# Order of 32-row groups per expert: 3, 3, 2, 2, 3, 3 in place of 3, 3, 2, 3, 3, 2

## The reference

```python
logits = (xt @ w_router) + b_router
top_val, top_idx = lax.top_k(logits, TOP_K)        # 4 of 32 experts for each token
gates = jax.nn.softmax(top_val, axis=-1)
...
hid = x_pad[toks] @ w1[e] + b1[e]                  # w1[e]: 1024 x 2048, float32, 8 MB
glu = jnp.minimum(hid[..., :D_FF], SWIGLU_LIMIT)
lin = jnp.clip(hid[..., D_FF:], -SWIGLU_LIMIT, SWIGLU_LIMIT)
act = glu * jax.nn.sigmoid(SWIGLU_ALPHA * glu) * (lin + 1)
y   = (act @ w2[e] + b2[e]) * wts[:, None]         # w2[e]: 1024 x 1024, float32, 4 MB
```

## Time and profile before

| | |
|---|---|
| median of three runs | 1705.96 us |
| the profiled execution's own time | 1706.75 us |
| its span (first to last instruction) | 1705.0 us |
| PE busy over the span | 1593.5 us, 93% |
| matmuls with w1 (line 2337), 5376 of them | 612.2 us busy, 61.5 idle before them |
| matmuls with w2 (line 2349), 5376 of them | 296.5 us busy, 1.8 idle before them |
| DMA, last slices before the end | 9 tenths or more busy, 403 to 430 GB/s |
| chain that ended last | PE 71%, DMA 26% |

### The profile page before, as it was taken

The page is one execution under the profiler, slowest core; times in us unless marked ns, Lnnn a source line. Parts: engine busy times, 40 slices in busy tenths (PEclk is TensorE's granted clock), DMA queues, the critical chain, the costliest instruction groups (busy, mean ns, idle before and its releaser), DMA issues.

```text
span 1705.0 us, 32935 instructions
## 1 busy us (share of the span) xinstructions
PE 1593.5 (93%) x14089; PEld 819.2 (48%) x14089; DVE 646.2 (38%) x1131; ACT 202.3 (12%) x434; POOL 369.4 (22%) x416
## 2 busy tenths in 40 slices
PE   7999999999999998999989898989899998989886
PEld 5776767566668855343433333433333333433334
DVE  5565457455463535541322221312213222313125
ACT  2211012222120011010000000000100000100001
POOL 1521122111027613212121121121211211211201
PEclk9999999999999998999999999999999999999999
DMA  7442434111125353899999999999999999999996
GB/s 261 147 136 70 145 101 105 45 37 52 37 100 141 112 234 142 316 404 420 427 424 427 421 422 407 410 422 430 421 404 427 425 426 403 415 427 426 423 428 268
DMA packets 91968, 498.19 MB, mean 292 GB/s; under 512 B 9280, under 2 KB 58672, under 8 KB 74000
## 3 DMA queue, kind: packets, MB, share of 16 engines
q1 hardware_dynamic: 78304, 463.06, 67.2%
q0 software_dynamic: 13040, 32.61, 5.6%
q10 hardware_dynamic: 496, 0.56, 0.1%
HBM read 477.56 MB, written 23.89 MB: 294 GB/s over the span
## 4 chain that ended last, share of the span: by engine, by line
PE 71%; DMA 26%; issue 1%; DVE 1%; SPq 0%; ACT 0%; POOL 0%; POOLq 0%; ACTq 0%; DVEq 0%
PE PS L2337 26%; DMA ring<-in_w 23%; PE PS L519 12%; PE PS L2349 6%; PE PS L2218 6%; PE PS L2123 3%; PE PS L2243 3%; PE PS L2083 3%; PE PS L2163 2%; PE PS L2047 2%; PE PS L2183 2%; DMA ring<-y_dram 1%; PE PS L2167 1%; PE PS L2152 1%; PE PS L1922 1%
## 5 line engine op out<-in xcount | busy, mean ns | idle before, releaser
L2337 PE MATMUL PS<-ring,mix_sb 128*32 128x512 f32 x5376 | 612.2, 614 | 61.5 <-DMA ring<-in_w 60.6
L2337 PEld LDWEIGHTS PS<-ring,mix_sb 128*32 128x32 f32 x5376 | 174.4, 113 | 481.6 <-issue 393.7
L2349 PE MATMUL PS<-ring,hm_sb 128*32 128x256 f32 x5376 | 296.5, 379 | 1.8 <-DMA ring<-in_w 1.8
L1804 DVE TENSOR_TENSOR low_sb<-PS,low_sb 128x1536 f32<-128x1536 f32 (+1 forms) x32 | 49.9, 1558 | 605.0 <-PE PS L2337 605.0
L2349 PEld LDWEIGHTS PS<-ring,hm_sb 128*32 128x32 f32 x5376 | 172.2, 110 | 133.6 <-issue 19.0
L965 POOL COPY ints<-ints 128x3 int32 (+1 forms) x30 | 5.6, 187 | 674.2 <-ACT hm_sb L1200 674.2
L1194 ACT ACTIVATE hm_sb<-hm_sb 128x768 f32<-128x768 f32 (+1 forms) x32 | 24.6, 767 | 709.8 <-DVE hm_sb L1806 709.8
L910 POOL DMA_INDIRECT mix_sb<-xt_dram,ints x84 | 86.6, 1031 | 63.9 <-POOL ints L952 23.0
L936 POOL DMA_INDIRECT y_dram<-hm_sb,ints x80 | 80.9, 1011 | 43.3 <-POOL ints L965 25.5
L519 PE MATMUL PS<-uT_sb,ring 128*128 128x512 f32 (+2 forms) x240 | 78.2, 483 | 0.0
L1817 DVE STREAM_TRANSPOSE hm_sb<-mix_sb 128x768 f32<-128x768 f32 (+1 forms) x32 | 45.3, 1414 | 84.1 <-PE PS L2349 84.1
(11 more groups left out here) (390 smaller groups left out, 1635.3 us busy)
## 6 DMA issues: line engine op xcount, KB each, us to landing
ring<-in_w SPq DMA_DIRECT2D x58, 4096.0 KB, 20.0
ring<-in_w SPq DMA_DIRECT2D x72, 2048.0 KB, 21.0
ring<-in_w_in SPq DMA_DIRECT2D x24, 512.0 KB, 5.4
ring<-in_w_in SPq DMA_DIRECT2D x8, 1024.0 KB, 5.3
y_dram<-at_sb POOLq DMA_DIRECT2D x4, 2048.0 KB, 10.8
ring<-in_w SPq DMA_DIRECT2D x8, 1024.0 KB, 5.1
ring<-y_dram SPq DMA_DIRECT2D x4, 2048.0 KB, 25.0
x_sb<-in_x SPq DMA_DIRECT2D x8, 512.0 KB, 8.7
```

The source lines that it names most:

```text
L1804: V.tensor_tensor(hid, PS[:, at:at + g, :], b1_row.unsqueeze(1).broadcast_to([P, g, 2 * QR]), ALU.add).then_inc(hid_used, 1)
L2337: last = nc.tensor.matmul(PS[32 * j:32 * j + 32, at + t, :].rearrange("p (c n) -> p c n", c=2), xgT[n][:, k, 32 * t:32 * t + 32], w1_c[k][ ...
L2349: last = nc.tensor.matmul(PS[32 * j:32 * j + 32, Y_BANK + t, 0:QR], actT[:, k, 32 * t:32 * t + 32], w2_in[k // 2][:, k % 2, j * QR:(j + 1) ...
```

## The change

Only the list of groups changes. There are still 20 positions of three groups and 12 of two, and the even and the odd places of six still hold eight groups each.

```diff
-GROUPS = [3, 3, 2] * 10 + [2, 2]
+GROUPS = [3, 3, 2, 2, 3, 3] * 5 + [2, 2]
```

## The result

The changed kernel takes 1710.7 us (median of 10 runs, 1709.39 to 1714.21), the kernel before 1706.77 us in the same comparison (10 runs). The ratio, taken over the runs that stood side by side, is 1.0029, 95% interval 1.0020 to 1.0039: 4.9 us slower, between 3.4 and 6.7 (the two medians alone are 3.9 us apart). The forecast was 1708.4 us, 2.5 us more than before; the measured time lies in its range, and the loss is about twice the one predicted. The same kernel run again gave 1.0030 (1.0018 to 1.0041).

What follows compares the result with a forecast made beforehand. Weight loads were taken to bound the expert part. Unchanged work gave 0 us, lateness behind three back edges 0 + 1.3 + 1.2 = 2.5 us; profiled 1706.75 + 2.5 = 1709.25, median 0.79 lower: 1708.4 us, range 1703.5 to 1716.

Steps and rivals of the forecast that it cites:

- What bounds: Expert part: weight loads set the pace, 30.7 to 31.3 us per expert against PE's average 27.7; sum of work changes 0 us.
- Where the loss comes from: Loop's back edges: the stall used to follow a 24.3 us step, now a 31.2 us step, so it is uncovered.
- Length of the stalls: PE's three back edges: stalls of 5.86, 5.51 and 5.42 us before, said to remain near 5.6 us.
- time in hand: Load queue behind each back edge: landing of the load ahead less next issue, 5.5, 6.2, 4.7 us; less 2.3: 3.2, 3.9, 2.4.
- Added lateness: PE at the back edges before steps 12, 18 and 24: 2.7, 4.8 and 3.2 us later than before.
- What lateness costs: Load queue behind the three back edges: costs only when the queue runs out; 0 + 1.3 + 1.2 = 2.5 us.
- uneven DMA engines: DMA engines at the back edges: the slowest sets the 31.3 us pace, idle time of quick ones is free; sum stays 2.5 us.
- third rival: Behind the back edges: one shared DMA limit, every idle us of quick engines lost, about 6 us each, 18 us, 1724; chance 0.04.
- second rival: Four 3-group steps around each edge: PE becomes the bound, 8 to 21 us in all, 1714 to 1727; chance 0.16.
- The first (no cost): All three back edges: the queue covers the lateness, time stays 1706.0 us; chance 0.25.
- The stall and its rule: Back edges: a taken branch outside the fetch window waits for its page by DMA, 5.4 to 5.9 us, whatever stood before it.
- Beginning and end: Positions 0 to 3 and the last steps: step 30 ends 3.5 us later before a wait; counted 0 us, at most 3.5.

## Why the prediction was right, and where it was short

- *What bounds.* Right: the loads set the pace, and the sum of the work is unchanged. The two orders without a loop agree, 0.9987 and 0.9988.
- *Where the loss comes from.* Right, and shown: the stall at the branch, which now follows a 3-group step. Taking the branch away, moving it behind the 2-group steps, or giving the queue more in hand each take the loss away.
- *Length of the stalls.* Right for the three back edges (5.1 to 5.4 us). One step failed, the count: the branch into the loop stalled too, 4.09 us in place of 0.84. The prediction read only the three back edges, though it named a stall at another place as a sign of being wrong; the 0.84 us before step 6 of the kernel before would have raised the question. By the count of branches it is worth up to 1.8 us, not settled. The time in hand fell most there, from 11.5 to 4.7 us.
- *Added lateness.* Foretold 2.7, 4.8 and 3.2 us; the time in hand fell by 0.5, 3.3 and 2.2. Step 12 came out much milder, the others 1.0 to 1.5 us milder.
- *What lateness costs.* This is the term of the sum that was mis-sized, and its mechanism was wrong. I let nothing cost as long as the slowest DMA engine had its next load 2.3 us ahead, and so came to 0 + 1.3 + 1.2. The time in hand stayed at 2.5 us or more for the first load behind every stall, and 4.9 us were lost. The 2.3 us were too long: the runs show 1.0 us from issue to first packet, and with that the prediction's own sum, in hand 5.5, 6.2 and 4.7 less 1.0 less the added 2.7, 4.8 and 3.2, is short nowhere and comes to 0. That the forecast of 2.5 us came as near as it did is luck: a term too large stood in for a cost that was left out.
- *The cost left out.* The part on uneven DMA engines said the idle time of the quick engines is free. It is not quite: the time rose while the slowest engine always had work. The engines' idle time in the mean went from 5.4 us to 7.4 and 8.3, and each is slow with its first packet (53 us of engine time for one MB in place of 37). The kernel before already paid about 2 us for its own branches, with 4.7 to 6.2 us in hand at its back edges. How the idle time of quick engines comes to delay the slowest one is not shown. The Trainium skill, "DMA: Bandwidth & Descriptors", section "Latency and other measured facts", says that two engines are usually slower. The profile does not tell the engines apart, so no run here shows which they are, and that two are slower does not make the others' idle time free, as I had concluded from it.
- *The third rival*, every idle microsecond of the quick engines lost, had 18 us (its own terms, 10.7 and three times 3.5, come to 21) and is wrong in size, but it named the right thing: the truth lies between it and the forecast. The second rival (PE bounds) is out: a load was in flight all the time. The first (no cost) is out by the interval.
- *The stall and its rule.* The Trainium skill, "Runtime: NRT & Kernel Launch", section "Instruction fetch mechanics", ties the stall to a taken branch. The runs agree: a stall of 4.9 to 6.2 us at each back edge was seen in every kernel with a loop and in neither without. A wait for weights in the same place does not shorten it (5.5 to 5.8 us in the kernel with the branch moved), but hides most of it from the time. So the prediction's "no order of steps hides it in a wait" holds for its length alone. What happens inside the stall no run here shows.
- *Beginning and end.* Right: step 31 still waits for its weights (3.89 us), so the longer `down` ahead of it is covered.

```profile
1643.58 8.77 PE L2337 MATMUL PS<-ring,mix_sb 128*32 128x512 f32 x64 [3.89 <-DMA ring<-in_w]
```

Left open: why the loads behind a stall are slowed by more than their share (33.5 us for the expert at step 18 with 2.9 us in hand), and whether the same DMA engine is the slow one throughout. No experiment here touched either.

The version without a loop is faster than both kernels, 1704.3 and 1704.9 us against 1706.3 (intervals 0.9978 to 0.9997), in either order.

## What to carry to other kernels

When a stall has a fixed place in the program, such as a loop's branch, ask what stands in front of it. Behind a short step it falls into a wait that is there anyway, behind a long one it delays the loads that the step would have released. Count every branch, the one into the loop too. A kernel in which a load is always in flight can still lose time to lateness, since most engines may be idle while the last one finishes, so compare share and GB/s behind the late place, and not only whether the next load was issued before the last one landed.

## What was not expected of the hardware

- The stall on entering the loop varies: 0.84 us in the kernel before, 3.49 and 4.09 in the changed one, 2.43 and 0.26 with the entry at positions 12 and 18. The same two 3-group steps stand ahead of it in the last four, so they do not set it, and what does is not shown. The back edges were 4.9 to 6.2 us in all kernels.
- DMA engines that start on a load after running out are slow with their first packet: 53 us of engine time for one MB from 1251 to 1252.5, then 37 us. The first packet starts 1.0 us after the issue.
- 4 MB loads in 2 MB pieces cost about 3 us over 28 experts (1.0018), although each was issued sooner and the GB/s from 740 to 1640 us did not fall (421 against 420).
